# Twelve more norm sums of an encoder trunk taken from one plain fp32 matmul each to two fp32r passes

## Chip, cores, metric

One core of a Trainium2 chip. The metric is the device time of one execution of the whole program, in microseconds (us). Three runs of the kernel before gave 2713.6, 2713.61 and 2713.67 us, median 2713.61.

## What is computed

Two layers of a bidirectional encoder over 1024 tokens of width 1024, all in fp32. Each layer normalises before and after every sub-layer:

```python
for i in range(DEPTH):
    h = rms_norm(x, g_pre_mix[i])
    z = h @ w_in[i]                       # q_a | kv_a | k_rope | B | C | conv_in
    ...                                   # latent attention, 8 heads
    conv = gate_b * short_conv(gate_c * conv_in, w_conv[i])
    mix = jnp.concatenate([group_rms_norm(attn, g_attn_out[i], N_HEADS),
                           group_rms_norm(conv, g_conv_out[i], CONV_GROUPS)], axis=-1)
    x = x + rms_norm(mix @ w_out[i], g_post_mix[i])
    hm = rms_norm(x, g_pre_mlp[i])
    f = jnp.square(jax.nn.relu(hm @ w_mlp_up[i])) @ w_mlp_down[i]
    x = x + rms_norm(f, g_post_mlp[i])
    gate = jax.nn.sigmoid(rms_norm(x, g_pre_ple[i]) @ w_ple_gate[i])
    x = x + rms_norm(gate * (p[i] @ w_ple_proj[i]), g_post_ple[i])
```

`rms_norm` multiplies by `rsqrt(mean(x*x) + eps)`, the mean taken over the channels of a token.

## The kernel before

Channels lie on the 128 partitions and tokens along the free dimension, in two halves of 512 tokens, t = 0 and 1. Large products are made of three fp32r passes, because each operand is kept as a high and a low fp32r part: high by high, high by low, low by high (lines 1135, 1137, 1136). One pass streams 128 x 512 values.

ACT makes high parts (`copy`, an ACTIVATE at line 1653), DVE makes low parts by subtraction (`low`, line 2147). Every engine runs its own list of instructions in the order written, and semaphores tie the lists together. PE, ACT and DVE each have a hand-written order for the mixing output and MLP part of a layer (`MIX_ACT`, `MIX_DVE`, `MLP_ACT`, `MLP_DVE`, steps named such as `copy_out.10` or `high.30`). PE calls its sums at the products named in `STATS_AT`.

A norm needs the sum of squares over partitions. ACT squares, DVE adds the chunks up into one tile of 128 x 512 (`add_square`, line 2177), and PE sums over partitions by a matmul with a matrix of ones; ACT then makes the factor (lines 1699 and 1701). The sum on PE comes in two forms. The plain form is one fp32 matmul on the total (line 1190 for norms ahead of a sub-layer, 1202 for those behind one, 1229 for the conv groups). The other, `two_passes` (lines 1174 and 1175), first has ACT copy the total into a high part (`high_of_total`) and DVE subtract it into a low part (`low_of_total`), and then streams both through PE as fp32r. The list `TWO_PASSES` says which border norms take the second form. `two_passes` waits for the low part.

The norms are named by kind, place k and half t: pre 0 is the norm ahead of the MLP, pre 1 ahead of the gate, post 0 behind the mixing, post 1 behind the MLP. So (post, 0, 0) is that behind the mixing for the first half.

In the input projection there are 36 outputs n = 0 to 35 of a layer, each 24 passes on PE. The conv branch takes 4 chunks j = 0 to 3 of 128 channels. For j under 3, at output n = `MULT_AT[j]` (15, 22, 29) DVE makes the taps and the gate and POOL multiplies by the norm factor (line 2667); at `MULT_AT[j]` + 1 (16, 23, 30) ACT squares the chunk into `cvs` (line 1750, `conv_squares`); behind the output `CSTAT_AT[j]` (17, 24, 31) PE takes the sum of both halves (`conv_stat`). For j under `TWO_PASS` ACT also writes the high parts `cvr_r`, and DVE the low parts `cvs_r`.

Output 30 is special. It is the rotary key `kr` for t = 1, and both engines handle it in a branch that stands ahead of the conv steps of the same n. ACT's code for n = 30, in its order:

```python
if kind == "kr":
    ...                                           # copy the output to sq
    for c in range(CHUNKS - 1):
        if MULT_AT[c] + 1 == n:
            conv_squares(L, c)
    act.wait_ge(kr_f, L * 2 + t + 1)              # DVE's rotated key
    for a in range(2):
        copy(kh[NOPE:P, a, hs(t)], kr[NOPE:P, :]).then_inc(kr_hi, 1)
...
for j in range(CHUNKS - 1):
    if MULT_AT[j] + 1 == n:
        ...
        for t2 in range(2 if j < TWO_PASS else 0):
            act.wait_ge(cv_sq, L * 8 + 2 * j + t2 + 1)
            copy(cvr_r[:, t2, :], cvs[:, t2, :]).then_inc(cv_sq_hi, 1)
```

DVE for n = 30 likewise first makes the key (lines 2315 to 2324), waits for each high part `kh`, subtracts the low parts `kl`, and only then comes to the low parts of the conv squares.

Of the kernel before, what the change touches and what calls it, by code (L numbers as in the profile page):

```python
# [163 lines left out]
CHUNKS = CONV // P  # L164
FIRST_AT = [0, 2, 4, 6]
WARM = 14
TWO_PASS = 2
TAIL_BANKS = (4, 5, 7, 0, 1, 2)


# [68 lines left out]
MIX_ACT = steps("""  # L239
copy_out.0 high.26 copy_out.1 square_out.0 copy_out.2 square_out.1 copy_out.3 high.27 square_out.2  # L240
square_out.3 copy_out.4 square_out.4 copy_out.5 square_out.5 copy_out.6 high.28 square_out.6 high.29
copy_out.7 square_out.7 copy_out.8 square_out.8 copy_out.9 square_out.9 high.30 post.0.0 copy_out.10
square_out.10 chunk.0.0.0 high.31 copy_out.11 chunk.0.0.1 square_out.11 high.32 copy_out.12 chunk.0.0.2
high.33 chunk.0.0.3 copy_out.13 high.34 chunk.0.0.4 copy_out.14 chunk.0.0.5 chunk.0.0.6 copy_out.15
chunk.0.0.7 high.35 pre_high.0.0 square_out.12 square_out.13 pre.0.0 square_out.14 high.36 hidden.0.0 square_out.15
high.37 post_high.0.1 hidden.0.1 high.38 post.0.1 hidden.1.0 chunk.0.1.0 high.39 hidden.1.1 chunk.0.1.1 chunk.0.1.2 copy.0
copy.1 copy.2 chunk.0.1.3 chunk.0.1.4 high.40 copy.3 copy.4 copy.5 chunk.0.1.5 chunk.0.1.6
chunk.0.1.7 copy.6 copy.7 high.41 pre.0.1
""")

MIX_DVE = steps("""
low.26 sum_out.1 low.27 sum_out.2 sum_out.3 sum_out.5 low.28 sum_out.6 low.29 sum_out.7 sum_out.8 sum_out.9
low.30 add_x.0.0.0 sum_out.10 add_x.0.0.1 chunk.0.0.0 add_x.0.0.2 low.31 add_x.0.0.3 chunk.0.0.1 add_x.0.0.4
low.32 add_x.0.0.5 sum_chunk.0.0.1 add_x.0.0.6 sum_out.11 add_x.0.0.7 low.33 chunk.0.0.2 sum_chunk.0.0.2
chunk.0.0.3 low.34 sum_chunk.0.0.3 chunk.0.0.4 sum_chunk.0.0.4 chunk.0.0.5 sum_chunk.0.0.5 chunk.0.0.6
sum_chunk.0.0.6 chunk.0.0.7 sum_chunk.0.0.7 low.35 pre_low.0.0 sum_out.12 sum_out.13 value.0.0 sum_out.14 low.36
# [1 line left out]
chunk.0.1.0 low.39 rest.1.1 add_x.0.1.2 chunk.0.1.1 add_x.0.1.3 chunk.0.1.2 add_x.0.1.4 sum_chunk.0.1.1  # L258
add_x.0.1.5 sum_chunk.0.1.2 add_x.0.1.6 chunk.0.1.3 add_x.0.1.7 low.40 chunk.0.1.4 sum_chunk.0.1.3
sum_chunk.0.1.4 chunk.0.1.5 sum_chunk.0.1.5 chunk.0.1.6 sum_chunk.0.1.6 chunk.0.1.7  # L260
sum_chunk.0.1.7 low.41
""")


# [25 lines left out]
group_part.25 group_part.26 group_part.27 group_unit.5 square_down.0.2 square_down.0.3 square_down.0.6 square_down.0.7  # L290
high.98 hidden.30.0 high.99 post.1.0 hidden.30.1 chunk.1.0.0 chunk.1.0.1 high.100 high.101 hidden.31.0 chunk.1.0.2
chunk.1.0.3 high.102 high.103 hidden.31.1 chunk.1.0.4 chunk.1.0.5 square_down.1.0 high.104 chunk.1.0.6 square_down.1.1
high.105 chunk.1.0.7 square_down.1.2 embed.0 high.106 embed.1 square_down.1.3 embed.2 high.107 embed.3 square_down.1.4
square_down.1.5 embed.4 embed.5 square_down.1.6 square_down.1.7 embed.6 embed.7 high.108 embed.8 embed.9 embed.10
high.109 pre.1.0 embed.11 embed.12 embed.13 embed.14 high.110 embed.15 high.111 post.1.1 chunk.1.1.0 high.112
chunk.1.1.1 chunk.1.1.2 gate.0 high.113 high.114 use.0 chunk.1.1.3 high.115 chunk.1.1.4 gate.1 chunk.1.1.5 use.1
gate.2 chunk.1.1.6 use.2 gate.3 chunk.1.1.7 gate.4 use.3 use.4 pre_high.1.1 gate.5 pre.1.1 use.5 gate.6 use.6 gate.7
use.7 high.116 post.2.0 gate.8 use.8 high.117 chunk.2.0.0 chunk.2.0.1 chunk.2.0.2 gate.9 high.118 chunk.2.0.3 gate.10
# [20 lines left out]
add_x.1.0.4 sum_chunk.1.0.2 sum_chunk.1.0.3 add.31.0 sum_chunk.1.0.4 add.31.1 add.31.2 add_x.1.0.5 add_x.1.0.6  # L319
add_x.1.0.7 sum_chunk.1.0.5 chunk.1.0.0 sum_chunk.1.0.6 add.31.3 sum_down.1.1 add.31.4 chunk.1.0.1 chunk.1.0.2 low.104  # L320
low.105 chunk.1.0.3 chunk.1.0.4 chunk.1.0.5 chunk.1.0.6 chunk.1.0.7 sum_chunk.1.0.7 add.31.5 low.106 sum_down.1.2
sum_down.1.3 low.107 add.31.6 sum_down.1.4 add.31.7 sum_down.1.5 sum_down.1.6 sum_down.1.7 low.108 low.109 low.110
low.111 add_x.1.1.0 add_x.1.1.1 z.0 add_x.1.1.2 low.112 chunk.1.1.0 add_x.1.1.3 sum_chunk.1.1.1 add_x.1.1.4
sum_chunk.1.1.2 add_x.1.1.5 add_x.1.1.6 low.113 add_x.1.1.7 low.114 y.0 chunk.1.1.1 chunk.1.1.2 chunk.1.1.3
sum_chunk.1.1.3 z.1 low.115 chunk.1.1.4 y.1 sum_chunk.1.1.4 z.2 chunk.1.1.5 sum_chunk.1.1.5 y.2 sum_use.1 z.3
# [89 lines left out]
    return (e[0] in ("high", "low") and e[1] >= LOADS) or e[0] == "in" or (e[0] in ("chunk", "sum_chunk", "pre") and e[1] == 2)  # L415


TWO_PASSES = [("pre", 0, 0), ("post", 0, 1), ("pre", 1, 1), ("pre", 2, 0), ("post", 2, 1)]


def squares_of(L, order):
# [45 lines left out]
def encoder(nc, x_in, w_units, w_head, p_in, gains, table, consts, out):  # L467
# [17 lines left out]
    with ctx:  # L485
# [394 lines left out]
        def total_at(L, kind, k, t):  # L880

            if L < 0 or (kind, k, t) not in TWO_PASSES or (L + 1 == DEPTH and k == 2):
                return 0
            return L * len(TWO_PASSES) + TWO_PASSES.index((kind, k, t)) + 1

# [246 lines left out]
        def _(pe):  # L1132
# [82 lines left out]
            for L in range(DEPTH):  # L1215
# [3 lines left out]
                def conv_stat(j, t):  # L1219
                    if j < TWO_PASS:  # L1220
                        pe.wait_ge(cv_sq_lo, L * 2 * TWO_PASS + 2 * j + t + 1)
                        if j:
                            pe.wait_ge(cv_ln, L * 8 + 2 * j + t - 1)
                        two_passes(ps[:, 4 + t, :], ones_r[:, 1, :], cvr_r[:, t, :], cvs_r[:, t, :]).then_inc(cv_stat, 1)
                        return
                    pe.wait_ge(cv_sq, L * 8 + 2 * j + t + 1)
                    if j:
                        pe.wait_ge(cv_ln, L * 8 + 2 * j + t - 1)
                    nc.tensor.matmul(ps[:, 4 + t, :], blocks, cvs[:, t, :], start=True, stop=True).then_inc(cv_stat, 1)
# [416 lines left out]
        def _(act):  # L1646
# [99 lines left out]
            def conv_squares(L, j):  # L1746

                for t in range(2):
                    act.wait_ge(cv_done, L * 6 + 2 * j + t + 1)
                    nc.scalar.activation(cvs[:, t, :], cv[:, hs(t)], ACT.Square).then_inc(cv_sq, 1)  # L1750
# [11 lines left out]
            for L in range(DEPTH):  # L1762
# [4 lines left out]
                for n in range(8 if L else 0, len(IN_OUTS)):  # L1767
# [38 lines left out]
                    for j in range(CHUNKS - 1):  # L1806
                        if MULT_AT[j] + 1 == n:
                            if kind != "kr":
                                conv_squares(L, j)
                            for t2 in range(2 if j < TWO_PASS else 0):  # L1810
                                act.wait_ge(cv_sq, L * 8 + 2 * j + t2 + 1)
# [330 lines left out]
        def _(dve):  # L2142
            V = nc.vector

            def low(dst, whole, high):

                return V.tensor_tensor(dst, whole, high.bitcast(f32), ALU.subtract)  # L2147
# [93 lines left out]
            for L in range(DEPTH):  # L2241
# [12 lines left out]
                def conv_gate(j):  # L2254
                    dve.wait_ge(tap, L * 12 + 3 * j + 3)

                    w = IN_SEQ.index(IN_KIND.index(("B", j)))
                    if taker_of(w) == "ACT":
                        dve.wait_ge(in_act, L * ACT_OUTS + outputs_of("ACT", IN_OUTS.index((w, 1)) + 1))
                    else:  # L2260
                        dve.wait_ge(in_dve, L * DVE_OUTS + DVE_OUTS)
                    V.tensor_tensor(cv[:, :], cv[:, :], bb[:, j % 2, :], ALU.mult).then_inc(cv_raw, 1)
# [18 lines left out]
                for n in range(8 if L else 0, len(IN_OUTS)):  # L2281
# [58 lines left out]
                    for j in range(CHUNKS - 1):  # L2340
                        if MULT_AT[j] == n:
                            conv_taps(j)
                            conv_gate(j)
                        if MULT_AT[j] + 1 == n and j < TWO_PASS:
                            for t2 in range(2):
                                dve.wait_ge(cv_sq_hi, L * 2 * TWO_PASS + 2 * j + t2 + 1)
                                low(cvs_r[:, t2, :], cvs[:, t2, :], cvr_r[:, t2, :]).then_inc(cv_sq_lo, 1)
# [460 lines left out]
```

## Time and profile before

| | |
|---|---|
| median of three runs | 2713.61 us |
| span of the profiled execution | 2712.5 us |
| granted TensorE clock over the span | 1.000 |
| PE busy | 2698.8 us, 99% |
| DVE busy | 2034.9 us, 75% |
| ACT busy | 1398.9 us, 52% |
| POOL busy | 302.7 us, 11% |

The span runs from the first to the last instruction of the one profiled execution. The median is 1.1 us above it, which is what lies around the span. Engines are PE (TensorE; PEld its weight load), DVE (VectorE), ACT (ScalarE), POOL (GpSimd) and SP (SyncE). In the timeline each line is a start, a length, engine, source line, operation and tiles; "idle before" is the engine's idle time ahead of it with what ended it. Passes on PE overlap in the records, so the cost of one is read from start to start.

### The profile page before, as it was taken

What the parts mean: (1) busy time and instruction counts of PE and PEld (TensorE: products, weight loads), DVE (VectorE), ACT (ScalarE), POOL (GpSimd) and SP (SyncE); (2) the same over time, 40 slices, a digit from 0 to 9 for tenths busy, and PEclk for the clock granted to TensorE, in tenths of its full rate; (3) what the DMA queues carried; (4) which work ended last, traced back from release to release, by engine and by line L of the source; (5) the groups of instructions that cost most, each with busy time, mean ns of one, the idle gap of its engine ahead of it and who ended that gap; (6) DMA issues with size and microseconds to landing.
All of it is one profiled execution on the core that took longest, in us unless ns stands there. A gap on an engine that the chain in (4) does not pass through costs nothing.

```text
span 2712.5 us, 34671 instructions
## 1 busy us (share of the span) xinstructions
PE 2698.8 (99%) x12854; PEld 2242.9 (83%) x12854; DVE 2034.9 (75%) x2758; ACT 1398.9 (52%) x2401; POOL 302.7 (11%) x329
## 2 busy tenths in 40 slices
PE   9999999999999999999999999999999999999999
PEld 7888888888888888888888888888888888888886
DVE  5468888476787777798866788893867787777986
ACT  5337888564333333356634478884633333333464
POOL 0230000001111111110003200000011111111000
PEclk9999999999999999999999999999999999999999
DMA  4221112531111111133232111133311111111422
GB/s 166 78 72 37 34 34 76 181 109 71 62 47 55 39 58 51 63 117 117 86 119 73 60 41 34 29 132 131 140 45 49 63 47 55 39 55 55 148 94 78
DMA packets 85943, 206.19 MB, mean 76 GB/s; under 512 B 8976, under 2 KB 37776, under 8 KB 84752
## 3 DMA queue, kind: packets, MB, share of 16 engines
q1 hardware_dynamic: 85776, 203.97, 22.3%
q8 instruction: 103, 1.69, 0.3%
q14 instruction: 64, 0.52, 0.1%
HBM read 172.42 MB, written 31.52 MB: 75 GB/s over the span
## 4 chain that ended last, share of the span: by engine, by line
PE 96%; DVE 2%; ACT 1%; DMA 0%; issue 0%; SPq 0%; ACTq 0%
PE ps L1135 28%; PE ps L1137 28%; PE ps L1136 28%; PE ps L1344 4%; PE ps L1369 2%; PE ps L1368 2%; DVE nm L2386 1%; PE ps L1174 0%; PE ps L1175 0%; DVE ptl L2393 0%; PE ps L1309 0%; PE ps L1202 0%; ACT hh L1653 0%; DVE wl L2147 0%; PE ps L1160 0%; PE ps L1161 0%
## 5 line engine op out<-in xcount | busy, mean ns | idle before, releaser
L1135 PE MATMUL ps<-hh,wh 128*128 128x512 f32 x2160 | 847.9, 393 | 1.4 <-DVE hl L2183 1.3
L1137 PE MATMUL ps<-hh,wl 128*128 128x512 f32 x2160 | 840.8, 389 | 0.0
L1136 PE MATMUL ps<-hl,wh 128*128 128x512 f32 x2160 | 840.7, 389 | 0.0
L1653 ACT ACTIVATE wh<-raw 128x256 fp32r<-128x256 f32 (+2 forms) x510 | 319.2, 631 | 443.2 <-PE ps L1137 314.5
L2147 DVE TENSOR_TENSOR wl<-raw,wh 128x256 fp32r<-128x256 f32 (+2 forms) x510 | 379.6, 757 | 159.0 <-ACT wh L1653 158.6
L1135 PEld LDWEIGHTS ps<-hh,wh 128*128 128x128 f32 x2160 | 405.6, 188 | 89.1 <-issue 3.6
L1136 PEld LDWEIGHTS ps<-hl,wh 128*128 128x128 f32 x2160 | 405.6, 188 | 86.9 <-issue 3.6
L1137 PEld LDWEIGHTS ps<-hh,wl 128*128 128x128 f32 x2160 | 405.5, 188 | 84.5
L2574 DVE TENSOR_TENSOR xf<-xf,ps 128x1024 f32<-128x1024 f32 x280 | 337.4, 1214 | 35.9 <-PE ps L1137 34.7
L1135 PE MATMUL ps<-hx,wh 128*128 128x512 f32 x448 | 174.4, 389 | 0.5 <-DVE xf L2574 0.5
L1137 PE MATMUL ps<-hx,wl 128*128 128x512 f32 x448 | 174.3, 389 | 0.0
L1136 PE MATMUL ps<-hx,wh 128*128 128x512 f32 x448 | 174.3, 389 | 0.0
L2393 DVE TENSOR_TENSOR ptl<-ps,pth 128x512 fp32r<-128x512 f32 x256 | 163.8, 680 | 9.4 <-ACT pth L1653 8.8
L1653 ACT ACTIVATE pth<-ps 128x512 fp32r<-128x512 f32 x256 | 140.5, 595 | 48.2 <-PE ps L1344 45.0
L2386 DVE TENSOR_REDUCE nm<-ps 128x1 f32<-128x1024 f32 x128 | 155.4, 1214 | 1.4 <-PE ps L1137 1.1
L1865 ACT ACTIVATE pr<-ps,nm 128x1024 f32<-128x1024 f32 x128 | 142.8, 1115 | 14.2 <-DVE nm L2386 12.4
L2700 POOL TENSOR_TENSOR spare<-raw 128x256 f32<-128x256 f32 x56 | 43.2, 771 | 872.3 <-DMA raw<-w_units 872.3
L1344 PE MATMUL ps<-cst,pr 128*128 128x128 f32 x1024 | 138.3, 274 | 1.2 <-DVE ptl L2393 1.2
L1344 PEld LDWEIGHTS ps<-cst,pr 128*128 128x128 f32 x1024 | 116.2, 140 | 15.5 <-issue 4.0
L1368 PE MATMUL ps<-pth,vv 128*128 128x256 f32 x512 | 128.1, 284 | 0.0
L1369 PE MATMUL ps<-ptl,vv 128*128 128x256 f32 x512 | 127.2, 283 | 0.0
L1690 ACT ACTIVATE sq<-xf 128x512 f32<-128x512 f32 x168 | 103.1, 623 | 45.0 <-DVE accy L2177 19.8
(241 smaller groups left out, 4303.3 us busy)
## 6 DMA issues: line engine op xcount, KB each, us to landing
raw<-w_units SPq DMA_DIRECT2D x170, 512.0 KB, 3.4
raw<-w_units SPq DMA_DIRECT2D x112, 256.0 KB, 2.9
x_mid<-xf SPq DMA_DIRECT2D x4, 2048.0 KB, 7.9
xf<-x_mid SPq DMA_DIRECT2D x4, 2048.0 KB, 7.7
hh<-mix_hi SPq DMA_DIRECT2D x14, 512.0 KB, 6.1
hl<-mix_lo SPq DMA_DIRECT2D x14, 512.0 KB, 7.0
stage<-w_head SPq DMA_DIRECT2D x16, 320.0 KB, 3.3
mix_hi<-cyh SPq DMA_DIRECT2D x8, 512.0 KB, 2.6
```

Source lines behind the costliest of these rows:

```text
L1135: nc.tensor.matmul(dst, ah, bh, start=start, stop=False)
L1136: nc.tensor.matmul(dst, ah, bl, start=False, stop=False)
L1137: return nc.tensor.matmul(dst, al, bh, start=False, stop=stop)
L1344: last = nc.tensor.transpose(ps[:, 4 + b, c * P:(c + 1) * P], pr[:, s % 2, (4 * b + c) * P:(4 * b + c + 1) * P], ident)
L1368: nc.tensor.matmul(dst, vv[:, a, c, V_DIM:3 * V_DIM], pth[:, G % 2, c, :], start=c == 0, stop=False)
L1369: last = nc.tensor.matmul(dst, vv[:, a, c, 0:2 * V_DIM], ptl[:, G % 2, c, :], start=False, stop=c == 7)
L1653: return nc.scalar.activation(dst, src, ACT.Copy, **more)
L1865: nc.scalar.activation(pr[:, s % 2, :], ps[:, 2 * (s % 2):2 * (s % 2) + 2, :].rearrange("p b n -> p (b n)"), ACT.Exp, bias=nm[:, s % 2:s % ...
L2147: return V.tensor_tensor(dst, whole, high.bitcast(f32), ALU.subtract)
L2386: V.tensor_reduce(nm[:, s % 2:s % 2 + 1], ps[:, 2 * (s % 2):2 * (s % 2) + 2, :].rearrange("p b n -> p (b n)"), AX.X, ALU.min).then_inc(s_l ...
L2393: V.tensor_tensor(ptl[at], ps[:, 4 + b, :].rearrange("p (c q) -> p c q", c=4), pth[at].bitcast(f32), ALU.subtract).then_inc(t_lo, 1)
L2574: V.tensor_tensor(f, f, ps[:, bank:bank + 2, :], ALU.add if sign > 0 else ALU.subtract).then_inc(down_add, 1)
```

## The change

Four more border norms of a layer join `TWO_PASSES`, (post, 0, 0), (pre, 0, 1), (pre, 1, 0) and (post, 1, 1), and the third conv chunk (j = 2) does too, as `TWO_PASS` goes from 2 to 3. ACT and DVE get a high step and a low step for each new norm in their hand-written orders. The places of the sums in PE's list do not move, nor do `MULT_AT` and `CSTAT_AT`.

```diff
-TWO_PASS = 2
+TWO_PASS = 3
...
 MIX_ACT = steps("""
...
-copy_out.7 square_out.7 copy_out.8 square_out.8 copy_out.9 square_out.9 high.30 post.0.0 copy_out.10
+copy_out.7 square_out.7 copy_out.8 square_out.8 copy_out.9 square_out.9 post_high.0.0 high.30 post.0.0 copy_out.10
...
-chunk.0.1.7 copy.6 copy.7 high.41 pre.0.1
+chunk.0.1.7 copy.6 copy.7 pre_high.0.1 high.41 pre.0.1
...
 MIX_DVE = steps("""
...
-low.30 add_x.0.0.0 sum_out.10 add_x.0.0.1 chunk.0.0.0 add_x.0.0.2 low.31 add_x.0.0.3 chunk.0.0.1 add_x.0.0.4
+post_low.0.0 low.30 add_x.0.0.0 sum_out.10 add_x.0.0.1 chunk.0.0.0 add_x.0.0.2 low.31 add_x.0.0.3 chunk.0.0.1 add_x.0.0.4
...
-sum_chunk.0.1.7 low.41
+sum_chunk.0.1.7 pre_low.0.1 low.41
...
-high.105 chunk.1.0.7 square_down.1.2 embed.0 high.106 embed.1 square_down.1.3 embed.2 high.107 embed.3 square_down.1.4
+high.105 chunk.1.0.7 square_down.1.2 embed.0 high.106 embed.1 square_down.1.3 embed.2 high.107 embed.3 pre_high.1.0 square_down.1.4
...
-high.109 pre.1.0 embed.11 embed.12 embed.13 embed.14 high.110 embed.15 high.111 post.1.1 chunk.1.1.0 high.112
+high.109 pre.1.0 embed.11 embed.12 post_high.1.1 embed.13 embed.14 high.110 embed.15 high.111 post.1.1 chunk.1.1.0 high.112
...
-sum_down.1.3 low.107 add.31.6 sum_down.1.4 add.31.7 sum_down.1.5 sum_down.1.6 sum_down.1.7 low.108 low.109 low.110
+sum_down.1.3 low.107 add.31.6 sum_down.1.4 add.31.7 pre_low.1.0 sum_down.1.5 sum_down.1.6 sum_down.1.7 low.108 low.109 post_low.1.1 low.110
...
-TWO_PASSES = [("pre", 0, 0), ("post", 0, 1), ("pre", 1, 1), ("pre", 2, 0), ("post", 2, 1)]
+TWO_PASSES = [("post", 0, 0), ("pre", 0, 0), ("post", 0, 1), ("pre", 0, 1), ("pre", 1, 0), ("post", 1, 1), ("pre", 1, 1),
+              ("pre", 2, 0), ("post", 2, 1)]
```

Over two layers that is 8 border sums and 4 conv sums, two pairs of halves.

## Rows read from the trace of the kernel before

**Rows 1.** The page: busy time by engine, and the chain that ended last.
```profile
PE 2698.8 (99%) x12854; PEld 2242.9 (83%) x12854; DVE 2034.9 (75%) x2758; ACT 1398.9 (52%) x2401; POOL 302.7 (11%) x329
...
PE 96%; DVE 2%; ACT 1%; DMA 0%; issue 0%; SPq 0%; ACTq 0%
```

**Rows 2.** PE's waits, longest and shortest of nine: total us, times, longest us.
```profile
PE ps L1135 <- ACT pr L1865: 1.8, 4, 0.5
...
PE ps L1135 <- DVE wl L2147: 0.2, 1, 0.2
```

**Rows 3.** Timeline of PE at a plain border sum (start and length in us).
```profile
549.45 0.39 PE L1137 MATMUL ps<-hh,wl 128*128 128x512 f32 x1
549.68 1.02 PE L1202 MATMUL ps<-accy,ones_r 128*128 128x512 f32 x2
...
550.77 0.40 PE L1136 MATMUL ps<-hl,wh 128*128 128x512 f32 x1
```

**Rows 4.** Timeline of PE around a border sum of two passes.
```profile
583.00 0.39 PE L1137 MATMUL ps<-hh,wl 128*128 128x512 f32 x1
...
583.90 0.39 PE L1136 MATMUL ps<-hl,wh 128*128 128x512 f32 x1
```

**Rows 5.** Timeline of PE at the plain sums of conv chunk 2, layer 0.
```profile
184.62 0.39 PE L1137 MATMUL ps<-hh,wl 128*128 128x512 f32 x1
184.84 1.88 PE L1229 MATMUL ps<-cvs,ones_r 128*128 128x512 f32 x4
...
186.79 0.40 PE L1136 MATMUL ps<-hl,wh 128*128 128x512 f32 x1
```

**Rows 6.** Timeline of PE around the two-pass sums of conv chunk 1, layer 0.
```profile
149.25 0.39 PE L1137 MATMUL ps<-hh,wl 128*128 128x512 f32 x1
...
150.62 0.39 PE L1136 MATMUL ps<-hl,wh 128*128 128x512 f32 x1
```

**Rows 7.** Timeline of DVE and ACT: readiness of border sums in layer 0, and one PE place.
```profile
545.73 0.69 DVE L2177 TENSOR_TENSOR accy<-accy,sq 128x512 f32<-128x512 f32 x1 [4.75 <-ACT sq L1690]
...
621.56 0.68 DVE L2177 TENSOR_TENSOR tmp<-tmp,sq 128x512 f32<-128x512 f32 x1
...
628.71 0.69 ACT L1699 ACTIVATE rpre<-ps,eps 128x512 f32<-128x512 f32 x1 [4.75 <-PE ps L1190]
...
1258.98 0.59 ACT L1653 ACTIVATE et<-ps 128x512 f32<-128x512 f32 x1
...
1262.39 1.02 PE L1202 MATMUL ps<-accy,ones_r 128*128 128x512 f32 x2
```

**Rows 8.** Timeline of ACT from output 30, layer 0.
```profile
183.53 0.63 ACT L1750 ACTIVATE cvs<-cv 128x512 f32<-128x512 f32 x1 [1.07 <-POOL cv L2667]
186.24 1.15 ACT L1653 ACTIVATE kh<-kr 64x512 fp32r<-64x512 f32 x2 [2.08 <-DVE kr L2324]
187.41 0.60 ACT L1653 ACTIVATE cc<-ps 128x512 f32<-128x512 f32 x1
```

**Rows 9.** Timeline of DVE at the same place.
```profile
186.90 1.29 DVE L2147 TENSOR_TENSOR kl<-kr,kh 64x512 fp32r<-64x512 f32 x2 [0.69 <-ACT kh L1653]
```

**Rows 10.** The same steps and PE's sum in layer 1.
```profile
1527.99 1.88 PE L1229 MATMUL ps<-cvs,ones_r 128*128 128x512 f32 x4
...
1530.05 1.29 DVE L2147 TENSOR_TENSOR kl<-kr,kh 64x512 fp32r<-64x512 f32 x2 [0.69 <-ACT kh L1653]
```

**Rows 11.** Timeline at conv chunk 0 of layer 1: ACT, DVE, PE.
```profile
1450.61 1.14 ACT L1653 ACTIVATE cvr_r<-cvs 128x512 fp32r<-128x512 f32 x2
...
1451.26 1.29 DVE L2147 TENSOR_TENSOR cvs_r<-cvs,cvr_r 128x512 fp32r<-128x512 f32 x2 [3.62 <-ACT cvr_r L1653]
...
1453.41 0.39 PE L1136 MATMUL ps<-hl,wh 128*128 128x512 f32 x1
```

**Rows 12.** Busy time by windows: PE, PEld, DVE, ACT, POOL, granted clock, DMA.
```profile
1.40:5.70 4.30, 4.22 (x10) 3.35 (x11) 0.06 (x4) 1.08 (x2) 0.00 (x0) 1.00 0.85 254
...
2707.50:2712.50 5.00, 0.00 (x0) 0.00 (x0) 0.53 (x1) 0.55 (x1) 0.00 (x0) 1.00 0.76 295
```

## The prediction

> **What bounds the kernel now.** I read the page first. PE is busy for 2698.8 of 2712.5 us and the chain that ended last is 96% PE [rows 1]; everything else is cover. Then PE's own waits: nine groups, the largest 1.8 us in all and none above 1.5 us at a time, together under 10 us [rows 2]. So a pass taken from PE is worth its full length, and a wait put in front of PE costs its full length, because nothing on PE can be done in its place: the list is served in order, and everything written behind the waiting sum stands. The question for each of the twelve sums is therefore only two things: what the two forms cost on PE, and whether the low part is there when PE arrives. The second I read from the timelines of ACT and DVE at each place, together with the order of the code.
>
> **What a border sum gives.** Matmul records overlap, so I measure from the start of the last product pass before the sum to the start of the second pass after it. With a plain sum in between this is 550.77 - 549.45 = 1.32 us [rows 3], with two passes 583.90 - 583.00 = 0.90 us [rows 4]. The difference is 0.42 us a sum. Eight sums (four places, two layers) give 8 x 0.42 = 3.36 us off the PE path. The low end is half of what a conv pair gains below, 0.40 us: 3.2 us.
>
> **Are the border totals split in time?** Each needs one ACT copy and one DVE subtraction. Bounds from the pairs of exactly these shapes: a pair of copies takes 1.14 us and a pair of subtractions 1.29 us, so one of each is at most 0.62 + 0.69 = 1.3 us in a row [rows 11].
> - (post, 0, 0): DVE's last addition ends at 545.73 + 0.69 = 546.42, and PE comes to the sum at 549.68 [rows 3, 7]. Ready at about 547.8, 1.9 us early. ACT and DVE stand idle there (the idle time ahead of DVE's addition is 4.75 us), so nothing queued is held up.
> - (pre, 0, 1): last addition ends at 621.56 + 0.68 = 622.24; PE's sum releases ACT's factor at 628.71, after 4.75 us of ACT idle [rows 7]. The sum itself starts about 1.1 us before that. Ready by 624.5, 3 us early. The step pushes the split of weight unit 41 by 0.6 us on each engine, into that same idle time.
> - (pre, 1, 0): the last addition (`sum_chunk.1.0.7`) stands five steps ahead of the low part in DVE's list, and the copy is written behind embed.3 while PE's sum stands behind embed.11. That is eight products of six passes, 8 x 6 x 0.227 = 10.9 us, against 1.3 us. It pushes the copies and squares behind it by 0.6 us on an engine that is 52% busy [rows 1]. I cost it at nothing; the cover is the slack of embedding copies, which have until four products later. Without cover it is at most 0.6 us a layer.
> - (post, 1, 1): here the place in the list decides, not the total. ACT's copy stands behind embed.12, which ends at 1258.98 + 0.59 = 1259.57; with 1.3 us the low part is ready at 1260.9, and PE comes at 1262.39 [rows 7]. It is 1.5 us early, and 1.1 us after PE has gained 0.42 us at the sum before.
>
> So all eight are covered, and the border part is -3.36 us, between -3.2 and -3.36 (to -2.0 with the one uncovered shift, 2 x 0.6).
>
> **What the conv sums give.** From pass to pass over both halves a plain pair takes 186.79 - 184.62 = 2.17 us [rows 5], the two-pass pair of chunk 1 takes 150.62 - 149.25 = 1.37 us [rows 6]. That is 0.80 us a layer, 1.6 us in all, if the parts are ready.
>
> **They are not ready.** Today the plain sum needs only ACT's squares, the last of which ends at 183.53 + 0.63 = 184.16 [rows 8], just ahead of PE at 184.84 [rows 5]. The new copies are written at the end of step n = 30, and n = 30 is the rotary key. ACT's next work behind the squares is not free: it waits 2.08 us for DVE's rotated key and then makes the two high parts `kh`, from 186.24 to 187.39 [rows 8]. Only behind them come the high parts of the conv squares. DVE in turn makes `kl` from 186.90 to 188.19 [rows 9] and only then the low parts.
>
> I lay the new steps on these times. ACT: the pair of copies starts at about 187.3 and takes 1.14 us [rows 11]; its first is done by 187.95, before DVE is free. DVE: the two subtractions follow `kl` at 188.1 (neighbouring records overlap by about 0.1 us) and take 1.29 us [rows 11], so they end at 189.39, the first at about 188.8. PE: at chunk 0 of layer 1 it already waited for such a pair. There the pair ended at 1451.26 + 1.29 = 1452.55 and the second product pass after the sums started at 1453.41, 0.86 us later [rows 11]. Carried over, that pass starts at 189.39 + 0.86 = 190.25 instead of 186.79 [rows 5]. The loss is 3.46 us, with the 0.80 us gain already inside it. PE stands still from about 184.85 to 188.85.
>
> In layer 1 all times are the same but for a shift: `kl` starts 2.06 us after PE's place (1530.05 against 1527.99) and in layer 0 also 2.06 us (186.90 against 184.84) [rows 5, 9, 10]. So 2 x 3.46 = 6.92 us.
>
> Who waits for that: PE's outputs 32 to 35 and all behind them. ACT and DVE get 1.2 to 1.3 us more work against a PE that is 3.46 us later, so they come out relatively earlier, and no second wait follows. DMAs come earlier relative to PE too. Whether some later wait of PE's shrinks by this is bounded by the under 10 us of all of them [rows 2], but what PE waits for there (a score's softmax, a key's low part) is started by PE's own outputs and moves along with them, so I take nothing.
>
> **The sum.** -3.36 + 6.92 = +3.56 us on a profiled span of 2712.5, which is 2716.1; with the 1.1 us between span and median, 2717.2 us. That is +0.13%. The ends of the small terms (-2.0 for the border part; each stall 0.3 us shorter or longer) give 2716.6 to 2719.2 at most, and most likely 2716.6 to 2718.0.
>
> **The rivals.**
> (a) No stall, the gain as meant. If the low parts of the third chunk were ready when PE comes, the sum is -3.36 - 1.6 = -5.0 us, 2708.7 us, -0.18%. For it speaks only that chunks 0 and 1 work this way in a place where little waits. Against it: at chunk 2 the squares themselves are ready just 0.7 us before PE, while copy and subtraction take 1.3 us or more even with both engines free.  The order behind the key is written in the code.
> (b) Slower by more than 0.2%: PE's clock falls during a stall. The standstill is about 4.0 us long, twice. The granted clock is 1.00 over the whole span, and at the end of the program it still reads 1.00 over 2707.50 to 2712.50, in which PE has no matmul at all [rows 12]. So a standstill of 5 us has been seen without a fall. The lower level is seen at the start: ten passes take 4.22 us from 1.40 to 5.70, 0.42 us each, close to twice 0.227: the 1.2 GHz level (the view prints 1.00 there, as its record begins with the first change) [rows 12]; at 2.4 GHz one takes (six from 149.25 to 150.62) about 0.227 us [rows 6]. If the clock fell once and took as long to come back as in that first stretch, ten passes would lose 10 x (0.42 - 0.227) = 1.9 us: 2719.1 us for one fall, 2721.0 for two. It decides from the point at which such a standstill is long enough. The Trainium skill, "TensorE: Matmul & The Clock Gate", section "What's actually happening", has it that "the default state is throttled, and activity releases the throttle", so an idle PE goes back to the lower level; by that rule this change, which lays two standstills into an unbroken stream, could lose its clock at both. The 5 us at the end speak against it here; one stretch doesn't settle it.
> (c) Only part of the stall, for instance because DVE's low parts of the key run earlier than laid out. A full stall is 3.46 + 0.80 = 4.26 us of delay a layer; half of it loses 2.13 - 0.80 = 1.33 us a layer, and the sum is -3.36 + 2.66 = -0.7 us, 2712.9 us. Nothing in the rows speaks for it.
>
> **How the numbers follow.** Forecast 0.75 (2716.6 to 2718.0), rival (b) 0.14, rival (a) 0.05, rival (c) 0.06. The predicted time is 2717.2 us. A range that leaves out at most 2 in 10 is the forecast with its bounds and the lower half of (b): 2715.8 to 2719.4. The measurement can tell about 0.2% from no change, 5.4 us. Faster by more than that (below 2708.2) needs (a) and a little more: 0.03. Slower (above 2719.0) is (b), with a little for longer stalls: 0.15. Within 0.2%: 0.82.
>
> **What would show it.** In the changed profile PE's waits should have a new group, line 1174 on DVE `cvs_r`, of about 4 us twice for the first half and some 0.3 us for the second. The eight border sums should show no PE wait and 0.9 us from pass to pass. ACT's `cvr_r` pair of chunk 2 should stand behind `kh`, at about 187.3 in layer 0. The granted clock should stay at 1.00. PE's busy time should fall by some 5 us while the span grows by 3.6. I am wrong if PE shows no wait at the third chunk (then the order on ACT or DVE isn't what I read), if border sums wait, or if the clock drops after one of the standstills.

## The result: slower by 8 us, with the clock falling in both standstills

| | median | span of the profiled execution |
|---|---|---|
| before | 2713.61 us (7 runs, 2713.22 to 2714.13) | 2712.5 us |
| after | 2721.58 us (7 runs, 2720.15 to 2723.4) | 2718.4 us (that run took 2720.15) |

The ratio after to before is 1.0030, 95% interval 1.0019 to 1.0041. The forecast was 2717.2 us, with a range of 2715.8 to 2719.4: the kernel is slower, and by more than the range allows. All seven runs lie above it. The profiled one is the fastest of them; its mean granted clock is 0.998, and the two slowest read 0.997.

The page of the changed kernel answers to [rows 1]. PE is busy 2.4 us less, where some 5 us had been forecast, while the span is 5.9 us longer:

```profile
PE 2696.4 (99%) x12854; PEld 2244.9 (83%) x12854; DVE 2043.8 (75%) x2770; ACT 1404.3 (52%) x2413; POOL 304.0 (11%) x329
...
PE 91%; DVE 6%; ACT 1%; issue 1%; POOL 0%; DMA 0%; SPq 0%; DVEq 0%; ACTq 0%
```

PE's waits (total us, times, longest us) answer to [rows 2]. The first and the eighth of ten are new. The first stands for the first half of the third chunk alone; the short wait of 0.3 us forecast for its second half didn't show:

```profile
PE ps L1175 <- DVE cvs_r L2148: 7.9, 2, 4.0
...
PE ps L1175 <- DVE sum_r L2148: 0.5, 2, 0.2
```

In the changed kernel every line number behind the diff is one higher: `two_passes` is lines 1175 and 1176.

The standstill is where the prediction laid it. ACT's timeline in layer 0 answers to [rows 8], with the new pair `cvr_r` behind `kh`:

```profile
183.31 0.63 ACT L1751 ACTIVATE cvs<-cv 128x512 f32<-128x512 f32 x1 [1.07 <-POOL cv L2668]
186.02 1.15 ACT L1654 ACTIVATE kh<-kr 64x512 fp32r<-64x512 f32 x2 [2.07 <-DVE kr L2325]
187.19 1.15 ACT L1654 ACTIVATE cvr_r<-cvs 128x512 fp32r<-128x512 f32 x2
```

DVE's answers to [rows 9], the new pair behind `kl`:

```profile
186.68 1.29 DVE L2148 TENSOR_TENSOR kl<-kr,kh 64x512 fp32r<-64x512 f32 x2 [0.69 <-ACT kh L1654]
188.00 1.29 DVE L2148 TENSOR_TENSOR cvs_r<-cvs,cvr_r 128x512 fp32r<-128x512 f32 x2
```

And PE's answers to [rows 5]. It stands for 3.96 us, takes the four passes of the sums and the first product pass at about full pace, and then does a pass every 0.43 us instead of every 0.23, until 193.56:

```profile
184.40 0.39 PE L1138 MATMUL ps<-hh,wl 128*128 128x512 f32 x1
188.75 0.50 PE L1175 MATMUL ps<-cvr_r,ones_r 128*128 128x512 f32 x1 [3.96 <-DVE cvs_r L2148]
...
190.18 0.63 PE L1137 MATMUL ps<-hl,wh 128*128 128x512 f32 x1
190.60 0.63 PE L1138 MATMUL ps<-hh,wl 128*128 128x512 f32 x1
...
193.56 0.40 PE L1136 MATMUL ps<-hh,wh 128*128 128x512 f32 x1
193.79 0.40 PE L1137 MATMUL ps<-hl,wh 128*128 128x512 f32 x1
```

Busy time by windows (PE, PEld, DVE, ACT, POOL, granted clock, DMA) names the reason. A value between 0.5 and 1.0 in the clock column means that the window holds some of each level. Behind the wait the granted clock falls to its lower level of 1.2 GHz for some 3.4 us, in layer 0 and in layer 1:

```profile
188.70:189.80 1.10, 1.05 (x4) 0.71 (x5) 0.91 (x2) 1.03 (x3) 0.00 (x0) 1.00 0.00 0
189.90:193.20 3.30, 3.30 (x10) 2.54 (x9) 0.41 (x1) 2.14 (x4) 0.00 (x0) 0.53 0.34 99
1534.60:1537.90 3.30, 3.30 (x8) 2.43 (x9) 1.36 (x2) 2.96 (x6) 0.00 (x0) 0.55 0.18 33
```

PE had already worked for more than 1.1 us when the clock fell in layer 0. The fall is put down to the standstill by the experiments below, not by this row alone.

### The profile page after: what moved, and what is told of

It is laid out like the page before. It is cut to its first block, busy times and chain, and to the rows that moved or that the text cites. A ratio compares the mean times of both kernels' runs of the same rounds, so it can differ in the third digit from the quotient of the medians.

```text
span 2718.4 us, 34699 instructions
## 1 busy us (share of the span) xinstructions
PE 2696.4 (99%) x12854; PEld 2244.9 (83%) x12854; DVE 2043.8 (75%) x2770; ACT 1404.3 (52%) x2413; POOL 304.0 (11%) x329
## 4 chain that ended last, share of the span: by engine, by line
PE 91%; DVE 6%; ACT 1%; issue 1%; POOL 0%; DMA 0%; SPq 0%; DVEq 0%; ACTq 0%
PE ps L1136 27%; PE ps L1138 27%; PE ps L1137 27%; PE ps L1345 4%; PE ps L1370 2%; PE ps L1369 2%; DVE wl L2148 1%; DVE nm L2387 1%; PE ps L1175 1%; PE ps L1176 1%; DVE xf L2575 0%; DVE xf L2202 0%; DVE ptl L2394 0%; PE ps L1310 0%; DVE hl L2184 0%
```

## Experiments

Each kernel was run beside the kernel before on the same chip. The median of before was 2713.76 us in the first group of four (the two parts of the change, 16 passes of filling, the sum moved), 2713.81 in the second (8 passes, the wait alone, the other order, both sums later) and 2713.9 in the last two (12 passes, three border sums); each group had a chip of its own.

**The two parts of the change by themselves.** The first kernel keeps only the border sums:

```diff
-TWO_PASS = 3
+TWO_PASS = 2
```

> The changed kernel with the third conv chunk back to its plain sums; the eight border sums stay in two passes. Theory (border sums gain 0.415 us each, but the later sum (pre, 1, 1) hangs on a chain of DVE and ACT that starts at the sum (post, 1, 1), so PE waits there and gives about 0.42 us back a layer): -3.3 + 0.85 = -2.5 us, 2711.1 us, with a PE wait on DVE sum_r of about 0.2 us twice and the granted clock at 1.00 throughout. Rival (all eight are covered, as forecast): -3.3 us, 2710.3 us, no such wait. Rival (border sums cost something that the trace doesn't show): above 2712.

Measured: 2710.77 us (11 runs, 2709.96 to 2711.95), ratio 0.9990 (0.9981 to 0.9998), clock 1.00. The border part gains, about 3 us, and PE waits on the low part `sum_r` at (pre, 1, 1), 0.8 us over the two layers. The second kernel is the kernel before with only the chunk:

```diff
-TWO_PASS = 2
+TWO_PASS = 3
```

> The kernel before with only the third conv chunk's sums in two passes. Theory (two standstills of 4 us, each followed by a stretch at the lower clock): 2 x 3.46 = 6.9 us for the standstills less the gain, and at least 2 x 1.7 = 3.4 us for the clock: 2713.6 + 10.3 = 2723.9 us, spread over some us from run to run. Rival (the clock falls cost nothing that matters): 2720.5 us.

Measured: 2723.36 us (5 runs, 2722.91 to 2725.48), ratio 1.0036 (1.0024 to 1.0049), with the same waits of 4.0 us and the same two falls of the clock. The third chunk alone costs 9.6 us; all of the loss is there.

**Standstill and clock taken apart.** The wait stays, but PE works through it, with passes on constant data. They go to PSUM bank 4, which the sum behind them overwrites; the wait on `cv_ln` makes sure that ACT has read the chunk before out of it:

```diff
+                    if j == 2 and t == 0:
+                        pe.wait_ge(cv_ln, L * 8 + 2 * j + t - 1)
+                        for _ in range(16):
+                            nc.tensor.matmul(ps[:, 4, :], ones_r[:, 0, :], ones_r[:, :, :].rearrange("p k m -> p (k m)"), start=True, stop=True)
                     if j < TWO_PASS:
                         pe.wait_ge(cv_sq_lo, L * 2 * TWO_PASS + 2 * j + t + 1)
```

> The changed kernel with 16 passes on constant data, read by nobody, in front of the wait for the third chunk's parts, so that PE works during most of the 4 us standstill (16 x 0.227 = 3.6 us). The wait ends when it did before. Theory (the idle PE makes the clock fall): the granted clock stays at 1.00 and the time falls by 3.4 us or more, to about 2717.5 us, with a spread as small as that of the kernel before. Rival (the clock falls for another reason, or costs little): 2721.6 us.

Measured: 2718.07 us (11 runs, 2717.63 to 2718.84), ratio 1.0016 (1.0007 to 1.0025). The sums start where they did before the filling, at 188.94 us; in the changed kernel it was 188.75, with all of PE's list 0.19 us earlier there. The passes behind them run at full pace. Timeline of PE:

```profile
184.59 0.39 PE L1138 MATMUL ps<-hh,wl 128*128 128x512 f32 x1
184.82 3.79 PE L1224 MATMUL ps<-ones_r 128*128 128x512 f32 x16
188.94 0.50 PE L1175 MATMUL ps<-cvr_r,ones_r 128*128 128x512 f32 x1 [0.34 <-DVE cvs_r L2152]
...
190.34 0.39 PE L1137 MATMUL ps<-hl,wh 128*128 128x512 f32 x1
...
199.20 0.39 PE L1137 MATMUL ps<-hl,wh 128*128 128x512 f32 x1
```

The same window as above in this kernel holds 16 passes instead of 10:

```profile
189.90:193.20 3.30, 3.30 (x16) 2.73 (x15) 0.61 (x1) 2.34 (x4) 0.00 (x0) 1.00 0.33 99
```

So 32 useless passes on constants make the program 3.5 us faster (2721.58 - 2718.07). That is the price of the two falls, 1.75 us each, and what is left, 2718.07, has the waits alone. It is close to the 2717.2 of the forecast and inside its range.

The traces give the price a second time. In the changed kernel the pass that stands at 199.20 above, the 41st product pass behind the sums, starts here:

```profile
200.63 0.39 PE L1137 MATMUL ps<-hl,wh 128*128 128x512 f32 x1
```

From the last pass before the sums that is 200.63 - 184.40 = 16.23 us, against 199.20 - 184.59 = 14.61: the fall cost 1.6 us in layer 0. The like stretch in layer 1 took 16.53 and 15.07 us, 1.5 us more. So the profiled execution, the fastest of its seven, paid 3.1 us, and the medians give 3.5.

**How long a standstill is long enough?** The same kernel with 8 passes of filling, and one with 12 (`range(12)`):

```diff
-                        for _ in range(16):
+                        for _ in range(8):
```

> The changed kernel with 8 instead of 16 passes on constant data in front of the third chunk's wait: PE works for 1.8 us of the 4 us and then stands for about 2.2 us. The place and end of the wait stay. If a standstill of 2.2 us is long enough for the clock to fall: about 2721.5 us, clock under 1.00. If it is too short: as with 16 passes, 2718 us. I expect the second; where it lies between, the clock falls in some executions only.

> The changed kernel with 12 passes on constant data in front of the third chunk's wait; PE then stands for about 1.25 us a layer. With 16 passes (0.34 us) the clock never fell, with 8 (2.15 us) in some executions. If 1.25 us is too short: 2718.1 us in all runs, clock 1.00. If not: a spread up to 2721. I expect the first.

Measured with 8: 2718.62 us (11 runs, 2717.57 to 2721.12), ratio 1.0019 (1.0010 to 1.0028). I had expected no fall, and was wrong for part of the runs: they spread from the level without falls up to that with two. The profiled run took 2720.78 us and its clock fell in both layers behind a standstill of 2.15 us. Its timeline of PE and its window behind the standstill:

```profile
184.73 1.98 PE L1224 MATMUL ps<-ones_r 128*128 128x512 f32 x8
188.86 0.50 PE L1175 MATMUL ps<-cvr_r,ones_r 128*128 128x512 f32 x1 [2.15 <-DVE cvs_r L2152]
```

```profile
189.90:193.20 3.30, 3.30 (x10) 2.54 (x9) 0.52 (x1) 2.25 (x4) 0.00 (x0) 0.51 0.35 99
```

Measured with 12: 2718.92 us (11 runs, 2717.73 to 2719.74), ratio 1.0018 (1.0009 to 1.0027), standstill 1.25 us, the clock at 1.00 in the profiled run. I had expected 2718.1 us in all runs.

The mean granted clock of each run tells more. One fall of 3.4 us at half the clock takes 0.0006 off the mean of a run, so a run that reads 1.000 had none. (A reading of 0.999 doesn't prove one, because the clock can also fall at the end of the program.) With 16 passes all eleven runs read 1.000, with 12 ten of eleven. With 8 four read 1.000, at 2717.57 to 2717.97 us, and seven 0.998 or 0.999, at 2718.0 to 2721.12. So it isn't falls that put the median with 12 above that with 16, and the intervals of the three don't separate them.

In this place, then, 0.34 us never made the clock fall, 1.25 us in no run but perhaps one, 2.15 us did in part of the executions, and 3.96 us did in both layers of the two kernels that have it (one profiled execution each; every run of both reads 0.997 to 0.999). Nor did the longest other wait of PE in these traces, 1.98 us near the start of the kernel with 16 passes, bring a fall: the passes behind it start 0.23 us apart, at 8.57, 8.80 and 9.03, and the clock is 1.00 from 4.50 to 20.00.

```profile
8.26 0.47 PE L1136 MATMUL ps<-hh,wh 128*128 128x512 f32 x1 [1.98 <-DVE hl L2188]
```

**The wait without the change.** The kernel before, its sums untouched, with one wait more:

```diff
+                    if j == 2 and t == 0:
+                        pe.wait_ge(kr_lo, L * 4 + 4)
                     pe.wait_ge(cv_sq, L * 8 + 2 * j + t + 1)
```

> The kernel before, its sums unchanged, with one more wait on PE in front of the third chunk's plain sums: for DVE's last low part of the rotary key. PE then stands for about 3.4 us a layer. Theory (what costs is the standstill behind the key, and the lower clock behind that; the form of the sums matters only by what it waits for): 2713.7 + 2 x 3.4 = 2720.5 us without clock falls, up to 2723.9 with a fall in each layer. Rival (a wait of this length is taken up elsewhere): below 2719.

Measured: 2724.33 us (5 runs, 2722.17 to 2724.94), ratio 1.0036 (1.0023 to 1.0050). PE stands for 3.24 us a layer behind the key's low part, and the clock falls there too, in both layers. Its waits, and its window behind the standstill in layer 0:

```profile
PE ps L1231 <- DVE kl L2149: 6.5, 2, 3.2
```

```profile
188.70:192.00 3.30, 3.30 (x6) 1.47 (x5) 0.83 (x1) 1.83 (x4) 0.00 (x0) 0.53 0.32 93
```

Neither the two-pass form nor the copies are needed for the loss. 2 x 3.24 = 6.5 us of waits and 2 x 1.75 = 3.5 us of clock make 10.0, and 10.5 was measured; the rest is inside the spread of its runs (2722.17 to 2724.94).

**The order behind the key.** PE's list is left alone; ACT makes each high part right behind its square, and DVE makes the low parts between the steps of the key. The edit on ACT (on DVE the two `low` steps go ahead of the waits for `kr_cos` and `kr_sum`):

```diff
-                                conv_squares(L, c)
+                                for t2 in range(2):
+                                    act.wait_ge(cv_done, L * 6 + 2 * c + t2 + 1)
+                                    nc.scalar.activation(cvs[:, t2, :], cv[:, hs(t2)], ACT.Square).then_inc(cv_sq, 1)
+                                    act.wait_ge(cv_sq, L * 8 + 2 * c + t2 + 1)
+                                    copy(cvr_r[:, t2, :], cvs[:, t2, :]).then_inc(cv_sq_hi, 1)
...
-                            for t2 in range(2 if j < TWO_PASS else 0):
+                            for t2 in range(2 if j < TWO_PASS and kind != "kr" else 0):
```

> The changed kernel with the third chunk's high parts made by ACT right behind each square, ahead of the rotary key's, and its low parts by DVE inside the key's chain; PE's list as in the changed kernel. Theory (the order behind the key makes the wait): the second low part is done about 1 us after PE comes, the standstill shrinks from 4 us to about 1 us, no clock fall: 2710.8 us (border part -2.5, chunk -0.3). Rival (the parts are late for another reason): near 2721.

Measured: 2711.11 us (11 runs, 2710.28 to 2712.75), ratio 0.9991 (0.9982 to 1.0001). Standstill 0.70 us, no fall. Timeline of PE:

```profile
184.97 0.49 PE L1175 MATMUL ps<-cvr_r,ones_r 128*128 128x512 f32 x1
185.30 0.40 PE L1176 MATMUL ps<-cvs_r,ones_r 128*128 128x512 f32 x1
186.40 0.50 PE L1175 MATMUL ps<-cvr_r,ones_r 128*128 128x512 f32 x1 [0.70 <-DVE cvs_r L2152]
```

The same work in another order on two engines is 10.5 us faster. It was the place behind the key.

**The sum moved instead of the parts.** One line on PE puts it behind output 32 instead of 31, 24 passes or 5.4 us later:

```diff
-                        if CSTAT_AT[j] == n:
+                        if CSTAT_AT[j] + (j == 2) == n:
                             conv_stat(j, 0)
```

> The changed kernel with PE's two sums of the third chunk written one output later in its list (behind output 32 instead of 31, 5.4 us later); ACT and DVE unchanged. Theory: the parts are ready at 189.4 us, PE comes at about 189.8, no standstill and no clock fall; 2713.6 - 3.3 + 0.85 - 1.6 = 2709.5 us. Rival (the later sum makes the conv chain late and PE waits further down, at the fourth chunk or the first keys): above 2711.

Measured: 2708.95 us (11 runs, 2708.01 to 2710.19), ratio 0.9982 (0.9973 to 0.9991). DVE's parts are made at the same time as ever, and PE comes 0.8 us behind them. DVE, then PE:

```profile
188.18 1.29 DVE L2148 TENSOR_TENSOR cvs_r<-cvs,cvr_r 128x512 fp32r<-128x512 f32 x2
```

```profile
190.01 0.39 PE L1138 MATMUL ps<-hh,wl 128*128 128x512 f32 x1
190.23 0.39 PE L1175 MATMUL ps<-cvr_r,ones_r 128*128 128x512 f32 x1
```

The conv chain behind it had room for the 5.4 us: in both kernels with this later sum no wait of PE on its factor or norm shows. This trace does have one wait of 0.79 us that the kernel before lacks, with no releaser that the profile shows:

```profile
483.13 0.47 PE L1136 MATMUL ps<-hh,wh 128*128 128x512 f32 x1 [0.79 <-issue]
```

The last kernel below has the same later sum and not this wait, so the move alone doesn't make it. What did isn't known.

**The small wait at (pre, 1, 1).** In every kernel here with all four new border sums, except the last one below, PE stands at (pre, 1, 1) for DVE's `sum_r`. That sum was in two passes before the change. My theory was that a chain of ACT and DVE runs from the sum (post, 1, 1) to it and is as long as PE's own work between them, so that shortening the first sum only makes PE early at the second. The test keeps the border sums only and takes the new form off (post, 1, 1), with its high and low step on ACT and DVE:

```diff
-TWO_PASSES = [("post", 0, 0), ("pre", 0, 0), ("post", 0, 1), ("pre", 0, 1), ("pre", 1, 0), ("post", 1, 1), ("pre", 1, 1),
+TWO_PASSES = [("post", 0, 0), ("pre", 0, 0), ("post", 0, 1), ("pre", 0, 1), ("pre", 1, 0), ("pre", 1, 1),
```

> The kernel with border sums only, and of these (post, 1, 1) back to its plain sum (three new border sums a layer, the third chunk plain). Theory (between the sums (post, 1, 1) and (pre, 1, 1) a chain of ACT and DVE sets the time, so what PE gains at the first it waits away at the second): PE's wait on DVE sum_r vanishes or shrinks to under 0.1 us, and the time is that of the kernel with four border sums, 2710.8 us, within some 0.2 us. Rival (the wait at (pre, 1, 1) comes from something else, such as the new copies ahead of it): the wait stays at 0.2 us or more, and the time is 0.8 us above the kernel with four.

Measured: 2710.59 us (11 runs, 2710.03 to 2711.85), ratio 0.9988 (0.9980 to 0.9997), against 2710.77 with all four. The wait is gone. PE at (pre, 1, 1) in layer 0 with four border sums, and then with three:

```profile
1299.77 0.39 PE L1138 MATMUL ps<-hh,wl 128*128 128x512 f32 x1
1300.68 0.47 PE L1175 MATMUL ps<-rpre_r,ones_r 128*128 128x512 f32 x1 [0.52 <-DVE sum_r L2148]
```

```profile
1299.75 0.39 PE L1138 MATMUL ps<-hh,wl 128*128 128x512 f32 x1
1299.98 0.44 PE L1175 MATMUL ps<-rpre_r,ones_r 128*128 128x512 f32 x1
```

Three sums a layer give what four give. The test took off two things at once, the shorter sum and the copies ahead of it, and copies on ACT and DVE could make `sum_r` late too. The timelines decide between them. First PE at (post, 1, 1) and DVE's low part for (pre, 1, 1) with the plain sum (three border sums), then with two passes (the changed kernel):

```profile
1260.99 1.02 PE L1203 MATMUL ps<-accy,ones_r 128*128 128x512 f32 x2
1299.10 0.69 DVE L2148 TENSOR_TENSOR sum_r<-tmp,rpre_r 128x512 fp32r<-128x512 f32 x1 [0.68 <-ACT rpre_r L1654]
```

```profile
1265.21 0.39 PE L1175 MATMUL ps<-rpre_r,ones_r 128*128 128x512 f32 x1
1303.31 0.69 DVE L2148 TENSOR_TENSOR sum_r<-tmp,rpre_r 128x512 fp32r<-128x512 f32 x1 [0.68 <-ACT rpre_r L1654]
```

The low part is done 38.80 us behind the start of the sum in one and 38.79 in the other. So neither the copies nor the shorter sum move it, and PE alone comes earlier, by what the sum gained. (In the kernel with border sums only it is 39.07 us in layer 0, and the wait 0.52 us; why it is 0.3 us later there isn't known.)

The last kernel has the third chunk's sums one output later and puts the sum (pre, 1, 1) three passes into gate product 7 instead of ahead of it:

```diff
-                    unit_output(bank, slot_of(GATE_UNIT[n]), t, ready).then_inc(gate_out, 1)
+                    between = (lambda: pre_stats(L, 1, 1)) if n == 7 else None
+                    unit_output(bank, slot_of(GATE_UNIT[n]), t, ready, between=between).then_inc(gate_out, 1)
```

(`between` is called behind the first three passes, and the entry of `STATS_AT` goes.)

> The kernel with the third chunk's sums one output later, and in addition PE's sum (pre, 1, 1) three passes later, inside gate product 7 instead of behind product 6. Theory (PE stands 0.4 us there for DVE's low part because the sum (post, 1, 1) before it became shorter and the chain between them did not): the wait on DVE sum_r goes, 0.8 us gained, 2708.1 us. Rival (ACT's factor comes later and the gate's second half waits): 2709 us or more.

Measured: 2708.21 us (11 runs, 2707.41 to 2708.99), ratio 0.9979 (0.9970 to 0.9988). The wait on `sum_r` is no longer among PE's waits. The two kernels with later sums were timed in different groups, and their intervals overlap, so that the last step gains is shown by the vanished wait rather than by the times. It is the fastest of all, 5.6 us below its own group's before.

## Why the prediction was wrong

**The bound: right.** PE is the path, and what is put in front of it costs its length. The bare wait shows it at full price.

**The stall: right in cause, place and size.** Forecast: PE stands from 184.85 to 188.85, `cvr_r` at about 187.3 behind `kh`. Measured: from 184.79 (184.40 + 0.39) to 188.75, `cvr_r` at 187.19. With the clock held, the second product pass behind the sums starts 190.34 - 184.59 = 5.75 us after the last pass before them, instead of 2.17 us: a loss of 3.58 us, where 3.46 was forecast. The other order on ACT and DVE, and the later sum on PE, both show that the order behind the key was the cause. Without falls of the clock the changed kernel takes 2718.07 us, where 2717.2 was forecast; it is the falls that took it out of the range.

**The clock: wrong, and this is the step that failed.** The fall was rival (b), with a chance of 0.14 and a price of 1.9 us each; it came in both layers and cost 1.75 us each. The price was nearly right and the chance was not. The working leaned on [rows 12]: no matmul from 2707.50 to 2712.50, clock 1.00. That is one stretch, at the end of a program, and it doesn't carry over. The end of the kernel with the sum one output later shows how little it bound. There the last matmul ends at 2702.60 + 0.21 = 2702.81. The second window reads 0.53, so all but about 0.2 us of it is at the lower level: the clock is down from about 2705.1, 2.3 us behind the last matmul (windows as above):

```profile
2702.60:2704.80 2.20, 0.21 (x1) 0.00 (x0) 0.79 (x2) 0.60 (x1) 0.00 (x0) 1.00 0.82 317
2704.90:2707.90 3.00, 0.00 (x0) 0.00 (x0) 0.00 (x0) 0.00 (x0) 0.00 (x0) 0.53 0.73 279
```

Within the one kernel with 8 passes, a standstill that measured 2.15 us in the profiled run came with falls in some runs and without in others. The rule cited from the Trainium skill ("TensorE: Matmul & The Clock Gate", "What's actually happening"), that idling takes the clock back to its lower level, was the better guide here than the single row set against it: every profiled standstill of 3.2 us and more in the middle of the program was followed by a fall, six of six in three kernels. The end of the kernel before is the one stretch that differs.

**The border sums: nearly right.** The 0.42 us a sum holds. Timeline of PE at (post, 0, 0) in the changed kernel, answering to [rows 3]: from the pass before the sum to the second pass behind it 554.51 - 553.60 = 0.91 us, where it was 1.32:

```profile
553.60 0.39 PE L1138 MATMUL ps<-hh,wl 128*128 128x512 f32 x1
553.83 0.39 PE L1175 MATMUL ps<-rpre_r,ones_r 128*128 128x512 f32 x1
554.05 0.39 PE L1176 MATMUL ps<-accy_r,ones_r 128*128 128x512 f32 x1
...
554.51 0.39 PE L1137 MATMUL ps<-hl,wh 128*128 128x512 f32 x1
```

All eight new sums found their parts ready, as forecast. What was missed is a sum that the change doesn't touch. I checked each new sum for its cover, and not the next sum down the list, which hung on a chain that now had less PE time beside it. The gain of (post, 1, 1) was given back at (pre, 1, 1). PE there in the kernel before, and then in the changed kernel:

```profile
1301.15 0.39 PE L1137 MATMUL ps<-hh,wl 128*128 128x512 f32 x1
...
1302.10 0.40 PE L1136 MATMUL ps<-hl,wh 128*128 128x512 f32 x1
```

```profile
1303.52 0.39 PE L1138 MATMUL ps<-hh,wl 128*128 128x512 f32 x1
1304.15 0.47 PE L1175 MATMUL ps<-rpre_r,ones_r 128*128 128x512 f32 x1 [0.24 <-DVE sum_r L2148]
...
1304.91 0.39 PE L1137 MATMUL ps<-hl,wh 128*128 128x512 f32 x1
```

From pass to pass it was 0.95 us and is 1.39. That is 0.9 us for two layers, a term of the sum that was left out.

**The sum again.** -3.4 for border sums, +0.9 given back, +6.9 for the standstills less their gain, +3.5 for the clock: +7.9 us, and +8.0 was measured. With the measured loss of 3.58 us a layer in place of the forecast 3.46 it is +8.2. The 3.5 in it is itself a difference of measured times; what the sum tests is the rest, +4.4 against the +4.5 of the kernel with filling. For two kernels without a standstill the same terms give 0.5 and 0.7 us less gain than measured (with border sums only -2.5 against -3.0, with the later sum -4.1 against -4.8). Where that remainder lies wasn't placed; it is smaller than the spread between runs, and the profiled spans with border sums only, 2710.1 against 2712.5 us, differ by 2.4.

**The other rivals.** (a), the gain as meant, is what the kernel with the later sum shows: 2708.7 was given for it, 2708.95 measured, but that needs PE's sum moved. That the two agree so closely is in part luck: the estimate lacks the 0.9 us given back, and the kernel gained the 0.7 us that no term holds. (c) didn't occur.

## What to carry to other kernels

Where PE is the path, a new wait on it has to be priced twice: its length, and a fall of the clock behind it. When the expected standstill is 3 us or more, take the fall as likely rather than as a tail; here 2.15 us was already enough in part of the runs. Moving the waiting step, or keeping PE at work in that time, was worth more than the saved passes. New steps written at the end of a shared step run behind everything else in it, on each engine that takes part. And when a step on the critical engine gets shorter, check the next wait on that engine, even one that the change doesn't touch.

## What was unexpected in the hardware

The lower clock came when PE was at work again: 1.1 us and more after the wait had ended in layer 0, about 0.3 us after it in layer 1 (0.55 over the 3.3 us from 1534.60 leaves 0.3 us at full clock). In layer 0 it lasted some 3.4 us. Passes that compute nothing and are read by nobody made the program 3.5 us faster by holding the clock at 2.4 GHz. And a standstill of 2.15 us led to a fall in some executions of the same kernel and in others not (2717.57 to 2721.12 us), while 1.98 us near the start of another led to none.
